# Attention in one pipeline: four passes of eight turns become one run of 34 turns in five steps

## What is computed

```
for gi, (wd, r) in enumerate(((128, 1), (512, 4), (2048, 16))):
    qi, ki, vi = qd[:, :, gi], kd[:, :, gi], vd[:, :, gi]    # rope(rms_norm(.)) of a slice of n @ w_in
    o, l = dilated_band(qi, ki, vi, r, wd // r)              # query t reads t - j*r, j = 0..wd/r
...
qm = rms_norm(q_m, mem_qn_g)
sm = einsum('bshd,bmhd->bhsm', qm, mem_k) * (MEM_HD ** -0.5)
om = einsum('bhsm,bmhd->bshd', softmax(sm), mem_v)
```

## Time and profile before

| | us |
|---|---|
| median of 3 runs | 5937.02 (5933.73 to 5939.94) |
| profiled execution | 5942.84 |
| its span | 5941.2 |

### The profile page before, as it was taken

One profiled execution on the slowest core, in us unless ns is written; L12 is line 12 of the kernel. 1 busy time (PEld: TensorE's weight loads), 2 busy tenths in 40 slices (PEclk: granted clock), 3 DMA queues, 4 the chain that ended last, 5 costly groups with the idle time before them and its releaser, 6 DMA issues. The chain is left out here.

```text
span 5941.2 us, 55349 instructions
## 1 busy us (share of the span) xinstructions
PE 4848.2 (82%) x17762; PEld 3079.4 (52%) x17762; DVE 2600.4 (44%) x5524; ACT 1804.7 (30%) x4697; POOL 1595.2 (27%) x1401
## 2 busy tenths in 40 slices
PE   7999999956644448987996888888888888888898
PEld 6888888856544338983433333333333333333353
DVE  2111111146344432102224666666666666666664
ACT  3111111123223221102222444444444444444433
POOL 0000000025334301001002444444444434444433
PEclk9999999965566565558998999999999999999989
DMA  7989888711132322235216999999999999999988
GB/s 251 298 272 307 270 281 268 235 62 56 57 98 83 87 59 110 101 124 218 95 55 274 421 421 421 421 421 421 420 419 416 416 416 411 418 414 414 406 356 355
DMA packets 315418, 1640.60 MB, mean 276 GB/s; under 512 B 41240, under 2 KB 85912, under 8 KB 173272
## 3 DMA queue, kind: packets, MB, share of 16 engines
q0 software_dynamic: 167344, 1179.45, 48.7%
q1 hardware_dynamic: 112416, 236.91, 11.8%
q10 hardware_dynamic: 35456, 221.91, 11.5%
HBM read 1551.85 MB, written 315.93 MB: 314 GB/s over the span
## 5 line engine op out<-in xcount | busy, mean ns | idle before, releaser
L2385 PE MATMUL ex_ps_y<-ex_rows,ex_diag 128*128 128x512 f32 (+1 forms) x4224 | 2028.3, 613 | 402.1 <-ACT ex_diag L2181 383.4
L2307 DVE CUSTOM_DVE_ANT_0 ex_rows<-ex_rows,ex_n2u 128x1024 f32<-128x1024 f32 x1056 | 1294.5, 1226 | 940.8 <-DMA ex_rows<-scratch_uv,ex_E 931.0
L2133 POOL DMA_INDIRECT ex_rows<-scratch_uv,ex_E x1056 | 1157.8, 1096 | 1723.1 <-PE ex_ps_y L2385 1493.4
L2385 PEld LDWEIGHTS ex_ps_y<-ex_rows,ex_diag 128*128 128x128 f32 (+1 forms) x4224 | 729.2, 188 | 1604.0 <-ACT ex_diag L2181 939.7
L307 PE MATMUL pj_ps<-pj_w_hi,pj_nT 128*128 128x470 f32 (+1 forms) x3456 | 784.2, 378 | 22.1 <-PE pj_ps L307 14.0
L307 PEld LDWEIGHTS pj_ps<-pj_w_hi,pj_nT 128*128 128x128 f32 (+1 forms) x3456 | 622.1, 181 | 149.5 <-issue 32.0
L2169 ACT ACTIVATE ex_gel<-ex_dots 128x1 f32<-128x1 f32 x1056 | 213.8, 202 | 1366.2 <-DVE ex_dots L2307 1365.1
L211 DVE COPY pj_zo<-pj_ps 128x470 f32<-128x470 f32 (+1 forms) x108 | 69.7, 645 | 897.6 <-PE pj_ps L307 752.8
L2181 ACT ACTIVATE ex_diag<-ex_ident,ex_w 128x128 f32<-128x128 f32 x1024 | 411.0, 401 | 50.8 <-PE ex_ps_y L2385 17.9
L307 PE MATMUL pj_ps<-pj_w_lo,pj_nT 128*128 128x470 f32 (+1 forms) x1728 | 406.3, 377 | 0.0
L211 ACT COPY pj_zo<-pj_ps 128x470 f32<-128x470 f32 (+1 forms) x108 | 59.6, 552 | 996.8 <-PE pj_ps L307 622.7
(11 more groups left out here) (362 smaller groups left out, 4651.0 us busy)
## 6 DMA issues: line engine op xcount, KB each, us to landing
pj_w<-in_w_in POOLq DMA_DIRECT2D x24, 1880.0 KB, 14.2
scratch_z<-pj_zo SPq DMA_DIRECT2D x192, 235.0 KB, 8.7
scratch_uv<-in_peer_u ACTq DMA_DIRECT2D x8, 4096.0 KB, 21.2
scratch_uv<-in_peer_v ACTq DMA_DIRECT2D x8, 4096.0 KB, 38.9
scratch_uv<-in_peer_u ACTq DMA_DIRECT2D x4, 8192.0 KB, 37.7
scratch_uv<-in_peer_v ACTq DMA_DIRECT2D x4, 8192.0 KB, 69.0
out_dk_s<-in_cache_dil_k ACTq DMA_DIRECT2D x8, 4088.0 KB, 44.4
out_dv_s<-in_cache_dil_v ACTq DMA_DIRECT2D x8, 4088.0 KB, 56.3
```

The lines of the kernel that those rows point to most:

```text
L2133: pool.indirect_dma_start(out=rows[:, p % SLOTS, :], out_offset=None, in_=d["uv"], in_offset=bass.IndirectOffsetOnAxis(ap=E[:, turn % 4, k ...
L2307: nc.vector.tensor_tensor_reduce(out=row, in0=row, in1=n2u[:, tile % 2], scale=1.0, scalar=0.0, op0=ALU.mult, op1=ALU.add, accum_out=dots[ ...
L2385: last = nc.tensor.matmul(y[0:n, 512 * c:512 * c + 512], diag[:, p % DIAGS, 0:n], rows[:, p % SLOTS, D + 512 * c:D + 512 * c + 512], start ...
```

## The change

`attend` does its work only in the call for group 0 and returns at once in the other three. That call now holds all turns of all four passes: 24 dilated ones (u = 0 to 23), two that make the memory keys (24 and 25) and eight that attend to the memory (26 to 33). They run in five steps, written out without loops: in step n, u = n is squared and summed, u = n-1 is scaled and turned by its angles, u = n-2 is transposed and scored, u = n-3 is masked and exponentiated, u = n-4 is transposed, multiplied by the values and stored.

`x` and `v` get three buffers instead of two; `stat`, `e`, `mx`, `nm`, `den`, `rden` and `lnd` get two instead of one; the memory keys and values have buffers of their own, so do the gains of the memory. `xr`, `t1`, `t2`, `tg`, `qT`, `pT` and the four PSUM tiles keep one. There are three fixed masks instead of a mask that is rewritten. A turn that has one key tile computes one tile (so the first turn of group 0 as well, and the zero fills of `kT` and `v` go). ACT now copies the whole of `pT`. The constants are loaded once, 12 DMAs and two for the memory values. POOL's wait for `y` of the turn before has moved from `t2` to `xr`. Waits are on constants, counted by `Count`.

```diff
+class Count:
+
+
+    def __init__(self, sem, turns, per=1):
+        self.sem, self.turns, self.per = sem, turns, per
+
+    def upto(self, turn):
+        return self.per * sum(1 for u in self.turns if u <= turn)
...
+    if group:
+        return
...
+    KEYS, ASK = NG * NT, NG * NT + MEM // P
+    N = ASK + NT
+    turns = range(N)
+    is_dil, is_key, is_mem = (lambda u: u < KEYS), (lambda u: KEYS <= u < ASK), (lambda u: u >= ASK)
+    dil, asking = [u for u in turns if is_dil(u)], [u for u in turns if not is_key(u)]
+    keyed = [u for u in turns if not is_mem(u)]
+    NX, NV = 3, 3
...
+        x, tab = sb("x", [P, NX, 2 * H, P]), sb("tab", [P, 2, 2, P])
...
+        sq, stat = sb("sq", [P, 2 * H, P]), sb("stat", [P, 2, 3, 2 * H])
...
+        y = sb("y", [P, 2, 2 * H, P])
+        qT, kT, kTm = sb("qT", [P, H, P]), sb("kT", [P, 2, H, P]), sb("kTm", [P, 2, H, P])
+        v, vm = sb("v", [P, NV, H, P]), sb("vm", [P, 2, H, P])
+        e, pT = sb("e", [P, 2, H, 2, P]), sb("pT", [P, H, 2, P])
+        mx, nm, den, rden, lnd = (sb(n, [P, 2, H]) for n in ("mx", "nm", "den", "rden", "lnd"))
...
-            step((0, 0, 0), None, None)
-            step((1, 0, 1), (0, 0, 0), None)
-
-            def two_steps(i):
-                for j in range(2):
-                    at = lambda lag: (i * 2 + (2 + j - lag), i + (2 + j - lag) // 2, (j - lag) % 2)
-                    step(at(0), at(1), at(2))
-
-            with eng.Fori(0, NT // 2 - 2) as i:
-                two_steps(i)
-            two_steps(NT // 2 - 2)
-            i = NT // 2 - 1
-            step(None, (2 * i + 1, i, 1), (2 * i, i, 0))
-            step(None, None, (2 * i + 1, i, 1))
...
+            load_x(1)
+            for n in range(LAST + 1):
+                if 2 <= n + 1 < N:
+                    load_x(n + 1)
+                if at(n, 3) is not None and is_dil(n - 3):
+                    load_v(n - 3)
+                if asks(n, 4) is not None:
+                    store_o(n - 4)
+                if at(n, 1) is not None and not is_mem(n - 1):
+                    store_y(n - 1)
...
+            def scaled(u):
+                after(pool, rs_done, u)
+                after(pool, x_in[u % NX], u)
+                after(pool, t1_done, u - 1)
+                after(pool, y_done, u - 1)
...
+            for n in range(LAST + 1):
+                if at(n, 1) is not None:
+                    scaled(n - 1)
+                    if is_dil(n - 1):
+                        crossed(n - 1)
+                if at(n, 0) is not None and is_dil(n):
+                    angles(n)
...
+                nc.scalar.copy(pT[:, :, w], ps_p[:, :, w]).then_inc(pT_out.sem, 1)
+
+            for n in range(LAST + 1):
+                if at(n, 0) is not None:
+                    squares(n)
+                if asks(n, 4) is not None:
+                    turned_weights(n - 4)
+                if at(n, 2) is not None:
+                    turned(n - 2)
+                if asks(n, 3) is not None:
+                    powers(n - 3)
+                if at(n, 0) is not None:
+                    roots(n)
...
-                nc.vector.memset(mask[:, 0, :], NEG).then_inc(masked, 1)
-                nc.vector.memset(kT[:], 0.0).then_inc(masked, 1)
-                nc.vector.memset(v[:, 1], 0.0).then_inc(masked, 1)
-                dve.wait_ge(masked, 3)
...
+                    m = mask[:, 2:3] if step_of(u) == 16 else mask[:, w]
...
+            for n in range(LAST + 1):
+                if asks(n, 3) is not None:
+                    masked(n - 3)
+                if at(n, 0) is not None:
+                    sums(n)
+                if at(n, 1) is not None and is_dil(n - 1):
+                    rotary(n - 1)
+                if asks(n, 4) is not None:
+                    output(n - 4)
+                if at(n, 1) is not None:
+                    rotated(n - 1)
...
+            for n in range(LAST + 1):
+                if asks(n, 4) is not None:
+                    turn_weights(n - 4)
+                if at(n, 2) is not None:
+                    turn(n - 2)
+                if asks(n, 4) is not None:
+                    values(n - 4)
+                if asks(n, 2) is not None:
+                    score(n - 2)
```

More of the change, by code:

```diff
@@ L993, in attend @@
[L993 to L996 removed]
+        consts_in, set_up, vm_in = sem("consts_in"), sem("set_up"), sem("vm_in")
+        x_in = [Count(sem(f"x_in{i}"), [u for u in turns if u % NX == i for _ in range(parts(u))], 16) for i in range(NX)]
+        tab_in = [Count(sem(f"tab_in{i}"), [u for u in dil if u % 2 == i for _ in range(parts(u))], 16) for i in range(2)]
@@ L1071, in back @@
-            def back(turn, i, j):
-                sp.wait_ge(out_done.sem, out_done.at(turn))
-                out = d["acts"][0:SEQ, 1536:2048] if memory else d["od"][group]
-                for p0, dst in rows(out, i, j):
-                    sp.dma_start(dst.rearrange("t (h e) -> t h e", h=H), o[p0:p0 + CLASS, j]).then_inc(o_stored[j], 16)
-                if not memory:
-                    sp.wait_ge(lse_done.sem, lse_done.at(turn))
-                    for p0, dst in rows(d["lse"][group], i, j):
-                        sp.dma_start(dst, lse[p0:p0 + CLASS, j, :]).then_inc(o_stored[j], 16)
@@ L1099, in _ @@
+            for i in range(2):
+                after(sp, y_stored[i], N)
+                after(sp, o_stored[i], N)
         @block.gpsimd
@@ L1344, in step, with turn_weights @@
-            def step(p, f, b):
-                if f:
-                    front(*f)
-                if b:
-                    back(*b)
-                    values(*b)
-            steps(pe, step)
+            pe.wait_ge(consts_in, 16 * N_CONSTS)
+            def turn_weights(u):
+                after(pe, e_done, u)
+                after(pe, pT_out, u - 1)
+                for h in range(H):
+                    for n in tiles(u):
+                        last = nc.tensor.transpose(ps_p[:, h, n, :], e[:, u % 2, h, n, :], ident[:])
+                last.then_inc(p_t.sem, 1)
@@ new lines, in turn, with values @@
+            def turn(u):
+                after(pe, y_done, u)
+                after(pe, qT_out, u - 1)
+                after(pe, kT_out, u - 1)
+                for h in range(heads(u)):
+                    last = nc.tensor.transpose(ps_t[:, h, :], y[:, u % 2, h, :], ident[:])
+                last.then_inc(t_done.sem, 1)
+            def values(u):
+                after(pe, pT_out, u)
+                if is_mem(u):
+                    pe.wait_ge(vm_in, 32)
+                else:
+                    after(pe, v_in[u % NV], u)
+                after(pe, out_done, u - 1)
+                for h in range(H):
+                    for n in tiles(u):
+                        val = vm[:, n] if is_mem(u) else v[:, (u - 1 + n) % NV]
+                        last = nc.tensor.matmul(ps_o[:, h, :], pT[:, h, n, :], val[:, h, :], start=(n == tiles(u)[0]), stop=(n == 1))
+                last.then_inc(o_done.sem, 1)
@@ new lines, in score @@
+            def score(u):
+                after(pe, qT_out, u)
+                after(pe, kT_out, min(u, ASK))
+                after(pe, sm_done, u - 1)
+                for h in range(H):
+                    for n in tiles(u):
+                        key = kTm[:, n] if is_mem(u) else kT[:, (u - 1 + n) % 2]
+                        last = nc.tensor.matmul(ps_s[:, h, n, :], qT[:, h, :], key[:, h, :], start=True, stop=True)
+                last.then_inc(scores.sem, 1)
+            for n in range(LAST + 1):
[7 more added lines that the diff above has]
+                    score(n - 2)
```

488 lines of the change are left out of this document (187 added, 301 removed).

## The result

The changed kernel took 5679.85 us (median of 4 runs, 5677.16 to 5681.94) against 5935.38 us (5932.98 to 5939.94), a ratio of 0.957 [0.955, 0.959]. Forecast were 5699 us with a range of 5660 to 5768. The profiled execution took 5677.16 us.

What follows compares the result with a forecast made beforehand. It took the latency of a chain over four engines, plus starts and ends, as the bound. Terms 21.5 + 202 + 59.5 + 16 + 3.3 = 302.3 us against 540.4 gave 5699 us, range 5660 to 5768.

Steps and rivals of the forecast that it cites:

- The base of 8.6: Dilated turns: `xr`, `t2`, `tg`, `t1` and `y` one after another cost 8.4 us, with handovers 8.6 a turn.
- if these five never overlap: Dilated turns: POOL's `xr`, `t2`, `tg` and DVE's `t1`, `y` exclude each other, 1.90 + 2.78 + 1.26 + 1.23 + 1.23 = 8.4 us.
- the circle: Dilated turns: `xr` waits for the previous `y`, `t2` for `xr`, `y` for `t2`; 5.9 us if overlap were free.
- The term for the clock: The 11 dilated turns with two tiles: PE, with one transpose group and one product slow, needs 9.0 us, not 8.6.
- Memory turns: Five memory steps: PE 5.6 us at full clock, 10.5 at the lower, `pT` wait 0.7; taken as 7.2 each, 36.
- The ends: Attention start: 20.1 us to the end of the first `y` as before, with three more constants 21.5.
- The drain: After the last `y`, the last turn runs from transposes to output: 13.8 to 18.4 us, taken as 16.
- Low clock: Rival (17%): PE's clock stays low, 11.4 + 0.2 us in 11 turns instead of 9.0, memory steps 10.7; 5747 us.
- DVE waits for POOL: Rival (15%): short DVE instructions also stop behind POOL, 3.3 us a turn, 10.8 instead of 8.8 in 23 steps; 5745 us.
- Better overlap: Rival (10%): everything overlaps better, 7.9 us instead of 8.8 in 23 dilated steps, 6.4 instead of 7.2 in memory; 5674 us.
- Closed within a turn: Rival (5%): a single buffer (`pT`, `ps_o`, `xr`) closes the waits within one turn, 12.8 us each; 5821 us.
- Fetch: Rival (3%, slower than before): fetching the written-out instructions sets PE's pace, 19.2 us a turn at 0.4 each; 6091 us.

## Why the prediction was right, and where its sizes were off

**The mechanism.** With the softmax chain in three steps the latency is gone from the turn, one- and two-tile turns take the same 8.20, and POOL in a steady turn has no idle time but 0.17 us behind `t2` and 0.08 ahead of it. The order does it: without it the turn is as long as before, or longer.

**The base of 8.6 was 0.4 too high, 9 us over 23 turns.** Together with the term for the clock below that is 13.6 us; the three uneven periods gave 0.6 back, which leaves the 13 between the two entries of the table. The step that failed is "if these five never overlap". POOL pays 2.33 - 1.26 = 1.07 us beside `y` and 3.78 - 2.78 = 1.00 beside `t1`, not 1.23 each. So a turn is 1.89 + 3.78 + 2.33 + 0.2 for the gaps = 8.20. The two rows with this overlap stood in the earlier trace rows (3.80 and a mean of 2.12), and the sum should have used them as they were: it gives 8.0. And the name was wrong in part: the forecast called it a circle, but the doubled buffers changed nothing. It is POOL that is full; the circle, and with two tiles DVE, are 0.8 to 0.9 us lower, as the run without `tg` shows.

**The term for the clock, 0.4 in 11 turns, was not needed, 4.4 us.** The granted clock was 0.84 with PE 69% busy, and PE keeps 2 us of idle time in a turn, in which a slow group or two fit.

**Memory turns** were put at 7.2 and took 5.81. PE of the changed kernel in one of them:

```profile
1926.05 2.05 PE L1294 MATMUL at_ps_o<-at_vm,at_pT 128*128 128x128 f32 x16 [0.66 <-ACT at_pT L1177]
1927.94 1.95 PE L1304 MATMUL at_ps_s<-at_kTm,at_qT 128*128 128x128 f32 x16
1929.73 1.04 PE L1273 MATMUL at_ps_p<-at_ident,at_e 128*128 128x128 f32 x8
1930.60 0.60 PE L1281 MATMUL at_ps_t<-at_ident,at_y 128*128 128x128 f32 x4
```

The clock was full (1.00), the wait for `pT` is 0.66 as forecast (0.7), and groups that follow each other overlap in the record by 0.15, so that 5.6 of PE is 5.15. The term that was too large is the 0.9 us for a clock below the full level. The first of the five steps took 6.64, the others 5.81, together 29.9 us for 36; the five around the keys took 1.5 us more than forecast. PE isn't full here, as the run with more transposes shows: what repeats is weights, copy of `pT`, values, scores.

**The ends.** 19.8 and not 21.5 to the first `y`. The three more constants cost what was forecast: the loads from `x` to the last mask are started over 6.1 us (1677.28 to 1683.37), where it was 4.7 (1680.17 to 1684.84). But SP starts the first of them 0.02 us ahead of the table load and not 1.7 behind it; the sum had no term for that, and why it starts earlier stays open. The drain came out at 16.1 for 16, in part by luck. Every group ran at the full level, for which the sum had 13.8; the rest is that the last turn's transposes and scores stand in PE's order behind groups of earlier turns, so that its scores began 4.2 us after its `y`, a wait that was not in the sum.

**SP.** That the third buffer of `x` covers late loads, worth 15 us, was wrong: with two buffers the time was 5680.2 us.

**The rivals.** *Low clock*: refuted. In the three windows above PE is 69%, 83% and 79% busy, at 0.84, 1.00 and, in the decode stage, again 0.50. Of the transposes: with eight more of them in each turn the clock over the dilated window was 0.91, not lower. The rule of the Trainium skill ("TensorE: Matmul & The Clock Gate", Part 4: PE-mode transpose) was not borne out as a limit for this kernel; the runs don't show what the chip counts. *DVE waits for POOL*: it happens, and costs nothing while POOL is full. Its mark is there (`nm` has a mean of 795 ns for 170, `t1` 1483 for 1305), in the groups of the changed kernel's attention (count | busy, mean ns of one | idle before):

```profile
L1213 DVE TENSOR_SCALAR at_nm<-at_mx 128x4 f32<-128x4 f32 x32 | 25.4, 795 | 1.1
L1225 DVE TENSOR_TENSOR at_t<-at_xr,at_tg 128x1024 f32<-128x1024 f32 x24 | 35.6, 1483 | 1.9 <-POOL at_xr L1103 1.9
```

But the waits of a turn with two tiles come to 0.43 + 0.27 + 0.36 = 1.1 us, not 3.3, and DVE had them to spare; with one tile they are 2.1 us, and its work is 1.1 us less. Of the three that the rival named, `rden` never waits: it takes 0.17 us in all 32 turns, 21 times beside POOL. That `nm`, with one input, ends when POOL's `xr` does agrees with the lock of the Trainium skill ("SBUF — State Buffer", SBUF: two separate sides). That page of the Trainium skill has the one who comes second stand for the whole of the other's instruction; POOL's stops here are 1.00 to 1.07 us for products of 1.23. *Better overlap*: half true, 8.2 against its 7.9. *Closed within a turn*: refuted, by the period. *Fetch*: refuted; over the whole attention PE's groups wait some 2 us for "issue", as the group of the scores shows:

```profile
L1304 PE MATMUL at_ps_s<-at_kT,at_qT 128*128 128x128 f32 x280 | 42.0, 307 | 4.4 <-issue 1.9 <-ACT at_kT L1156 1.3 <-ACT at_qT L1154 1.2
```

## What to carry to other kernels

Where no engine is full and each stands idle for another inside a step, try first to cut the chain in the step into more steps. Then sum each engine's turn with the durations it has beside its neighbours, not those it has alone: here the fullest engine by that sum set the new period. Once it was full, only work taken from it counted: more buffers changed nothing, more work on DVE or PE left the steady turn as it was or added 0.3 us to some, while POOL's table made once gave 15 us more. Then the next limits were close: the circle, DVE, and a load that came late because it stood behind another in the queue. Before moving such work into an earlier stage, look at what else its engine hands out there: 10 us were lost to a load of weights that was queued behind it. And an idle time that a profile puts down to "issue" can be a DMA that lands late: compare the start with the landing.

## What the runs showed of the hardware that was not expected

- A DVE product of two SBUF tensors (1.23 us) stops POOL for 1.00 to 1.07 us. Who is first goes on, the other stands: with `y` 0.04 us ahead `tg` takes 2.33 and `y` 1.23; with `tg` 0.07 us ahead, `tg` takes 1.26 and `y` 2.27.
- `nm`, on four columns, takes 0.17 us alone, but with POOL's `xr` at work 0.60 in the turns with two tiles and 1.65 in those with one; `lse` takes 0.15 alone and up to 1.26 behind `tg`. Not every DVE instruction waits: `rden`, also on four columns, stays at 0.17, the reduces at 1.22 (128x1024), and the mask out of PSUM at 1.22 beside POOL. Such a duration in the trace is partly a wait, and DVE "95% busy" still had room for a copy of 0.69 us a turn.
- In the run with more transposes the same DVE and POOL work has two steady turns: 8.20 where `y` comes before `tg`, and 8.52 where `tg` comes first and `lse` and `y` behind it. In the changed kernel too `tg` comes first in two turns where group 0 passes into group 1 (`y` takes 2.02 us and then `lse` 1.25), and then `y` is first again. What moves it from one to the other stays open.
